# Dense value tiles fetched in pairs, and a rotation of four gather buffers in place of five

## The reference

```python
# expert: (chunk, 8 heads, 16) indices, gate: their softmax weights
u = jnp.take(peer_u, expert, axis=0)
act = jax.nn.gelu(jnp.einsum('chkd,cd->chk', u, zc))
v = jnp.take(peer_v, expert, axis=0)
w = (gate * act.astype(jnp.float32)).astype(zc.dtype)
return jnp.einsum('chk,chkd->cd', w, v).astype(zc.dtype)
```

## Time and profile before

| | us |
|---|---|
| median of 3 runs | 2670.79 (2670.49 to 2677.07) |
| span of the profiled execution | 2671.2 |
| from the first dense matmul to the last | 2281.7 to 2659.0 |
| PE / DVE / ACT / POOL busy, share of the span | 84% / 79% / 43% / 24% |

### The profile page before, as it was taken

How to read it: one execution, slowest core, us unless ns; L and a number is a source line. 1 busy time by engine, 2 the same in 40 slices (tenths; PEclk the granted TensorE clock), 3 DMA queues, 4 the chain that set the end, 5 groups by cost and what they waited for, 6 DMA issues and landing times.

```text
span 2671.2 us, 32182 instructions
## 1 busy us (share of the span) xinstructions
PE 2250.8 (84%) x11476; PEld 1809.5 (68%) x11476; DVE 2099.3 (79%) x2971; ACT 1146.8 (43%) x1721; POOL 639.4 (24%) x834
## 2 busy tenths in 40 slices
PE   8999989999999999989999964444555558999997
PEld 7997778888888888879888841111222225777776
DVE  6986647665566556578766999989999999999997
ACT  5433554443444344453542110000355444548876
POOL 1000000000000000000001353542444442786663
PEclk9999999999999999999999976555677778999999
DMA  6534344555555555545558999999999995899996
GB/s 226 179 129 110 111 157 158 188 189 188 189 188 188 185 186 183 168 128 173 165 167 343 422 420 419 420 419 420 419 417 409 420 418 208 347 405 409 409 409 271
DMA packets 314517, 732.02 MB, mean 274 GB/s; under 512 B 21040, under 2 KB 223024, under 8 KB 275760
## 3 DMA queue, kind: packets, MB, share of 16 engines
q0 software_dynamic: 73728, 402.69, 37.1%
q1 hardware_dynamic: 240544, 327.03, 35.9%
q10 hardware_dynamic: 144, 1.05, 0.1%
HBM read 728.61 MB, written 2.10 MB: 274 GB/s over the span
## 4 chain that ended last, share of the span: by engine, by line
DVE 23%; PE 17%; DMA 13%; issue 3%; POOL 2%; ACT 1%; DVEq 0%; SPq 0%; ACTq 0%; PEldq 0%; POOLq 0%
DVE row L2497 12%; DMA row<-in_peer_u,expert 8%; DMA row<-in_peer_v_rows,expert 5%; PE pg L1294 4%; PE pl L865 4%; PE pl L872 3%; DVE pl L2513 2%; POOL row L801 1%; PE pl L868 1%; PE pl L869 1%; DMA v_tile<-in_peer_v_dense 1%; PE pg L1285 1%; PE pl L1259 1%; PE pl L1188 1%; POOL spread_lo L776 1%
## 5 line engine op out<-in xcount | busy, mean ns | idle before, releaser
L1957 DVE TENSOR_TENSOR wlo<-raw,whi 128x1024 fp32r<-128x1024 f32 (+1 forms) x436 | 517.9, 1208 | 374.9 <-ACT whi L1341 373.3
L1341 ACT ACTIVATE whi<-raw 128x1024 fp32r<-128x1024 f32 (+1 forms) x436 | 444.6, 1039 | 412.0 <-PE pl L872 407.2
L2497 DVE CUSTOM_DVE_ANT_0 row<-row,pg 128x2048 f32<-128x2048 f32 x256 | 574.7, 2284 | 34.0 <-DMA row<-in_peer_u,expert 32.3
L1259 PE MATMUL pl<-row,diag 128*128 128x512 f32 x404 | 316.7, 930 | 333.6 <-DMA row<-in_peer_v_rows,expert 297.8
L865 PE MATMUL pl<-x_split,whi 128*128 128x512 f32 x1888 | 478.5, 395 | 10.2 <-DVE x_split L1965 5.3
L1259 PEld LDWEIGHTS pl<-row,diag 128*128 128x128 f32 x404 | 101.1, 276 | 500.2 <-issue 445.2
L865 PEld LDWEIGHTS pl<-x_split,whi 128*128 128x128 f32 x1888 | 341.5, 190 | 74.6 <-issue 7.5
L872 PE MATMUL pl<-x_split,wlo 128*128 128x256 f32 x2656 | 373.7, 284 | 3.9 <-DVE wlo L1957 3.9
L872 PEld LDWEIGHTS pl<-x_split,wlo 128*128 128x128 f32 x2656 | 359.0, 192 | 23.1 <-DVE wlo L1957 4.5
L801 POOL DMA_INDIRECT row<-in_peer_u,expert x256 | 242.8, 949 | 367.1 <-DVE dots L2497 155.7
L801 POOL DMA_INDIRECT row<-in_peer_v_rows,expert x256 | 261.4, 1021 | 199.4 <-DVE dots L2497 67.0
(11 more groups left out here) (348 smaller groups left out, 3041.6 us busy)
## 6 DMA issues: line engine op xcount, KB each, us to landing
v_tile<-in_peer_v_dense SPq DMA_DIRECT2D x128, 512.0 KB
raw<-in_w_in SPq DMA_DIRECT2D x51, 1024.0 KB
raw<-in_w_gate SPq DMA_DIRECT2D x44, 1024.0 KB
raw<-in_w_up SPq DMA_DIRECT2D x44, 1024.0 KB
raw<-in_w_out SPq DMA_DIRECT2D x32, 1024.0 KB
raw<-in_w_down SPq DMA_DIRECT2D x32, 1024.0 KB
wq<-in_peer_wq SPq DMA_DIRECT2D x15, 1024.0 KB, 11.5
raw<-in_w_down SPq DMA_DIRECT2D x16, 768.0 KB
```

Source lines behind the costliest of these rows:

```text
L1259: last = mm(pl_all[:, c:c + width], diag[:, (at - 1) % 4, :], row[b][:, c - DENSE:c - DENSE + width], start=at == 1, stop=at == ADDED_ROWS ...
L1341: return nc.scalar.activation(o, i, ACT.Copy)
L1957: V.tensor_tensor(wlo[:, n % 4, 0:k, :], w[:, :, f, :], whi[:, n % 4, 0:k, :].bitcast(F32), ALU.subtract)\
L2497: V.tensor_tensor_reduce(row[b][:], row[b][:], z_tok[:], 1.0, 0.0, ALU.mult, ALU.add, dots[:, at:at + 1])\
```

## The change

The dense tiles are read two at a time: 64 transfers of 128 partitions x 2048 float32 (8 KB for each partition, 1 MB each), into three pair buffers that hold six tiles. The table in memory is laid out so that the two tiles of a pair stand next to each other for each partition. One semaphore stands for both tiles of a pair. A pair's buffer is loaded again once PE has finished both of its tiles. To make room, the buffer at `("arena", 3 * D)` leaves the rotation of gathered rows, which has four buffers in this stretch; the homes of `v_hi` move.

```diff
-           43: range(13, 17), SCATTERED: range(17, 18), LATER: range(18, 23)}
+           43: range(13, 17), SCATTERED: range(17, 18), LATER: range(18, 22)}
-ROWS_ALL = 23
+ROWS_ALL = 22
-TILE_HOMES = RING + 1
+PAIR_HOMES = 3
+TILE_HOMES = 2 * PAIR_HOMES
-        homes = [*(("xhi", m * GATHERED) for m in range(4)), ("arena", 3 * D)]
+        homes = [("xhi", m * GATHERED) for m in range(4)]
-        tile_homes = [("arena", 2 * D), ("arena", 3 * D + DENSE), ("arena", 4 * D), ("arena", 4 * D + DENSE),
-                      ("rest", choice_at)]
-        high_homes = [("arena", 2 * D + DENSE), ("rest", choice_at + DENSE), ("rest", choice_at + 2 * DENSE)]
+        pair_homes = [("arena", 2 * D), ("rest", choice_at), ("arena", 4 * D)]
+        tile_homes = [(region, start + h * DENSE) for region, start in pair_homes for h in range(2)]
+        high_homes = [("arena", 3 * D), ("arena", 3 * D + DENSE), ("rest", choice_at + 2 * DENSE)]
-        tile_full = [*slot_full, x_in[0]]
+        pair_full = slot_full[0:PAIR_HOMES]
-            for m in range(NKEY):
-                if m == 2:
+            for q in range(NKEY // 2):
+                if q == 1:
                     sp.wait_ge(hot_used, TT * GROUPS)
                     sp.wait_ge(row_added, ADDED_ROWS)
-                elif m >= TILE_HOMES:
-                    sp.wait_ge(tile_used, m - TILE_HOMES + 1)
+                elif q >= PAIR_HOMES:
+                    sp.wait_ge(tile_used, 2 * (q - PAIR_HOMES + 1))
-                sp.dma_start(v_tile[m % TILE_HOMES][:], A["peer_v_dense"][m]).then_inc(tile_full[m % TILE_HOMES], 16)
+                sp.dma_start(v_pair[q % PAIR_HOMES][:], A["peer_v_dense"][q]).then_inc(pair_full[q % PAIR_HOMES], 16)
-                act.wait_ge(tile_full[m % TILE_HOMES], tile_landed(m))
+                act.wait_ge(pair_full[m // 2 % PAIR_HOMES], tile_landed(m))
-    a["peer_v_dense"] = v[:, 0:DENSE].reshape(NKEY, NKEY, DENSE).transpose(1, 0, 2)
+    v_dense = v[:, 0:DENSE].reshape(NKEY, NKEY // 2, 2, DENSE)
+    a["peer_v_dense"] = v_dense.transpose(1, 0, 2, 3).reshape(NKEY // 2, NKEY, 2 * DENSE)
```

More of the change, by code:

```diff
@@ L99 @@
 ROWS_AT = {0: range(2), 2: range(2, 4), 8: range(4, 6), 20: range(6, 7), 24: range(7, 9), 31: range(9, 11), 37: range(11, 13),
-           43: range(13, 17), SCATTERED: range(17, 18), LATER: range(18, 23)}
+           43: range(13, 17), SCATTERED: range(17, 18), LATER: range(18, 22)}
 ROWS_LEFT = {SCATTERED: (4, 5, 6, 7, 8, 11, 12, 13, 14), LATER: range(18)}
 ROWS_FREE = {2: 1, 8: 2, 20: 4, 24: 5, 31: 6, 37: 7, 43: PH}
-ROWS_ALL = 23
+ROWS_ALL = 22
 ROWS_FROM = {}
-ROWS_SIGNAL = [*range(18), *ROWS_LEFT[SCATTERED][0:5]]
+ROWS_SIGNAL = [*range(18), *ROWS_LEFT[SCATTERED][0:4]]
 def row_buffers():
@@ L347, in build @@
         spread = [spread_all[:, t, 0:NKEY * P].rearrange("p (i c) -> p i c", i=NKEY) for t in range(TT)]
-        tile_homes = [("arena", 2 * D), ("arena", 3 * D + DENSE), ("arena", 4 * D), ("arena", 4 * D + DENSE),
-                      ("rest", choice_at)]
-        high_homes = [("arena", 2 * D + DENSE), ("rest", choice_at + DENSE), ("rest", choice_at + 2 * DENSE)]
-        v_tile = [sb(f"v_tile{m}", region, start, [P, DENSE]) for m, (region, start) in enumerate(tile_homes)]
+        pair_homes = [("arena", 2 * D), ("rest", choice_at), ("arena", 4 * D)]
+        tile_homes = [(region, start + h * DENSE) for region, start in pair_homes for h in range(2)]
+        high_homes = [("arena", 3 * D), ("arena", 3 * D + DENSE), ("rest", choice_at + 2 * DENSE)]
+        v_pair = [sb(f"v_pair{m}", region, start, [P, 2 * DENSE]) for m, (region, start) in enumerate(pair_homes)]
+        v_tile = [v_pair[m // 2][:, m % 2 * DENSE:(m % 2 + 1) * DENSE] for m in range(TILE_HOMES)]
         v_lo = [sb(f"v_lo{m}", region, start, [P, DENSE], F32R) for m, (region, start) in enumerate(tile_homes)]
@@ L533, in tile_landed @@
         def tile_landed(m):
-            n = m % TILE_HOMES
-            earlier = max(LOADS[u] for u in range(len(LOADS)) if u % RING == n) if n < RING else 1
+            n = m // 2 % PAIR_HOMES
+            earlier = max(LOADS[u] for u in range(len(LOADS)) if u % RING == n)
             return 16 * (earlier + m // TILE_HOMES + 1)
@@ L686, in _ @@
             sp.wait_ge(row_added, EARLY)
-            for m in range(NKEY):
-                if m == 2:
+            for q in range(NKEY // 2):
+                if q == 1:
                     sp.wait_ge(hot_used, TT * GROUPS)
                     sp.wait_ge(row_added, ADDED_ROWS)
-                elif m >= TILE_HOMES:
-                    sp.wait_ge(tile_used, m - TILE_HOMES + 1)
-                if m == GAIN_AT:
+                elif q >= PAIR_HOMES:
+                    sp.wait_ge(tile_used, 2 * (q - PAIR_HOMES + 1))
+                if 2 * q == GAIN_AT:
                     sp.dma_start(gain_all[:], A["norm_f_g_2"].rearrange("(a n) -> a n", a=1).broadcast_to([P, D])).then_inc(gain_in, 16)
-                sp.dma_start(v_tile[m % TILE_HOMES][:], A["peer_v_dense"][m]).then_inc(tile_full[m % TILE_HOMES], 16)
+                sp.dma_start(v_pair[q % PAIR_HOMES][:], A["peer_v_dense"][q]).then_inc(pair_full[q % PAIR_HOMES], 16)
             for t in range(TT):
```

## The result

The changed kernel takes 2713.84 us (median of 5 runs, 2705.12 to 2719.88) where the kernel before takes 2670.98 (5 runs): a ratio of 1.0152, with an interval of 1.0137 to 1.0168. By the ratio that is 41 us slower (the medians differ by 43), and outside the predicted range of 2661 to 2693. The profiled execution of the changed kernel took 2705.12 us, 8.7 us less than its median; its span is 2703.3 us, 32.1 us more than that of the profiled execution before.

The account below looks back on a forecast made before the run. The DMA engines were taken to bound the dense stage's long part, PE 2% and DVE 7% behind. 2671.2 - 3.7 (packets) + 2.0 (lumps) gave 2669.5 us profiled, a median of 2669; range 2661 to 2693.

Parts of the forecast that it names:

- Packet size: Dense tile loads: 8 KB packets move at 421 GB/s against 409 for 4 KB, saving 3.7 us on the path.
- A pair lands in 5.3 us: Pair loads: a pair lands about 5.3 us after issue, well inside the 8.8 us allowed; cost 0.
- Two thirds for the pair: Shared DMA engines: packets alternate between queues, so a moving pair gets two thirds; row gathers still fit, only lumpier.
- The landing shrinks with the queue: Four row buffers: landing is mostly queueing, falling from 9.4 to about 7 us, with the DMA engines still setting the pace.
- 2 us for lumps: Dense stage: DMA idle brought by lumpier timing, taken as a doubling of today's gap; 2 us slower.
- The start of the stage: First rows and pair of the dense stage: PE delayed about 1 us, then caught up; cost 0.
- B: Four row buffers: a row's landing stays above 7.9 us and sets the pace; 2692 to 2727 us, chance 0.08.
- A: DVE's row sums: DVE starves for rows while a pair is moving; 19 us slower, 2688 us, chance 0.18.
- The signs: Dense stage profile: DMA share clearly under 1, or over 12 us of PE gaps, would prove the forecast wrong.

Follow-up runs that it names:

- e8: Changed kernel with a fifth row buffer from the 15th row on and a fourth pair buffer from pair 12 on; 2682.92 us.
- e12: e9 with each pair moved as two transfers of 4 KB for each partition on one semaphore; 2677.36 us.
- e9: Changed kernel with a fourth pair buffer from pair 12 on and row buffers growing from four to seven; 2679.61 us.
- e3: Changed kernel with each pair loaded by two 4 KB-per-partition transfers, issued together on the pair's one semaphore; 2711.31 us.
- e11: e2 with two tiles issued at the same moment, each keeping its own 4 KB transfer and semaphore; 2697.65 us.
- e2: Changed kernel's memory map and four row buffers, but six single tiles, each with its own transfer and semaphore; 2690.32 us.
- e13: e10 with each pair moved as two transfers of 4 KB for each partition on one semaphore; 2701.47 us.
- e10: Changed kernel with a fourth pair buffer from pair 12 on, keeping its four row buffers; 2715.77 us.
- e1: Kernel before with four row buffers in the last stretch instead of five, tiles left single; 2689.36 us.
- e4: Changed kernel with the fifth row buffer given back from the 15th row on; 2683.96 us.

## Why the prediction was wrong, step by step

- **Packet size: -3.7 us, wrong.** Pairs did move as 64 transfers of 1024 KB, but no kernel with 8 KB packets moved the predicted 412 to 416 GB/s; the best (e8) had 409 in its long part, where the kernel before had 407. The 421 GB/s of the earlier trace rows were read in a stretch in which one queue did nearly all (q0 has 94.4% of the engines' time from 1500 to 1540 us), so packet size was not the only thing that differed from the dense stage; which of the two made the 421 was not tested. Over half of the traffic here is rows of 4 KB, and e12 against e9 prices the larger packet at no gain.
- **A pair lands in 5.3 us, so it costs 0: wrong.** It landed in 7.4 to 8.5 us on the chain, and ACT's wait grew to 98.9 us instead of shrinking. I costed a pair alone in its queue. But a pair is issued every 6.5 us (2 x 3.23) and needs more than that to land, so it stands behind the one before (argued from these numbers, not tested). Waiting for both halves costs 12 us (e3 against e11); issuing them at once costs 0 to 7 (e11 against e2, not shown).
- **Two thirds for the pair: right as a mechanism, unpriced.** That packets are taken from both queues in turn was read from the earlier trace rows. In the changed kernel the split is not quite two to one: from 2450 to 2453 us q1 (pairs) had 58.8% and q0 (rows) 40.0%. And e13 against e10 shows what that does to the rows: 14 us. I wrote that the sum fits and only the timing is lumpier, and left it at that.
- **The landing shrinks with the queue, the pace stays the engines': the step that failed most.** Of its two halves one held: for single tiles I put 2.6 to 3.1 MB in flight and e1 had 2.8. The other did not. "Still far from an empty queue" had no row behind it. With 2.8 MB the engines moved 389 GB/s, with 2.1 MB 331. A landing of "about 7 us" was 7.8 (median of all rows) in e1, 8.2 on its chain and 8.9 on that of the changed kernel, while the rule of the loop allows 7.65. I also took one landing time for both queues, though rows land 1 us later than tiles (7.8 and 6.8 in e1), and it is the rows that were short.
- **2 us for lumps: mis-sized.** It was the only term of the sum for the lost row buffer and the lumps together. In its place stand 15 us for the lost buffer with single tiles (e1) and 28 with pairs (the changed kernel against e4); 13 us are the pairs' own with five row buffers (e4), and all together are 41.
- **The start of the stage: 0 was wrong** in that what it lost was not made up: PE ran 256 matmuls in the second part against 292, three tiles, 9 us. The reason given (the DMA engines are the bound, so it is caught up) fell with the bound.
- **The rivals.** B was the one that happened, and its own formula would have given it: at 8.88 us a row takes (8.88 + 1.3) / 4 = 2.55 us, 36 us over 152 rows, so 2707 us; the median is 2714, the profiled span 2703. I gave it 0.08, since it was weighed by the same reckoning of the queue as the forecast, so an error there hit both. Its threshold of 7.9 us was also 0.25 too high: POOL's 0.26 us to issue was missing from it, and that alone decided little, as e1 was at 8.2. A's mechanism is there too: DVE waited 49.8 us for rows, at the edge of the 50 that A asked for, and its point, rows held back while a pair moves, is what e13 shows. A and B are one loop: A lengthens the landing, B turns it into time. Taken as separate cases they had 0.26 between them.
- **The signs.** The text named a DMA share clearly under 1 and over 12 us of gaps of PE as proof against it. Both came: 0.97 and 24 us in the long part.

## What to carry to other kernels

When a rotation of buffers gets one shorter, write down the loop: which work stands between one buffer's landing and its next issue, and how many items pass in a turn. Here five rows pass in the landing time plus 3.9 us. Then put in two landing times: the one of now (9.4 us gives 2.66 us a row, 53 us more: the worst) and the one hoped for (7 us gives 2.18, no cost). The truth lay between, at 15 us with single tiles and 41 with pairs. When the two ends decide differently, as here, the forecast must not rest on the hoped one. A change that enlarges the transfers of one queue has to be priced for the other queue that shares the engines, above all if that one has just lost a buffer. The lost buffer alone cost 15 us, the pairs alone (with five or more row buffers) 8 to 13, and both together 41.

## What the runs showed of the hardware

- The DMA share near 1 does not say that the engines are at their rate. In e1 it is 1.00 at 389 GB/s, in the kernel before 1.02 at 407, in the changed kernel 0.97 at 373. Only GB/s beside it tells.
- Transfers of 1 MB were no faster in total than those of 512 KB, with the rows beside them: e9 with 1 MB transfers took 2679.61 us, e12 with 512 KB 2677.36. The Trainium skill (DMA: Bandwidth & Descriptors, "Anatomy of one DMA", for DMAs issued by GpSimd) has a fixed time of about 2 us for each DMA, by which fewer and larger ones would be better. No run here shows that gain; that it is hidden because several transfers are always in flight is my reading, not tested.
- PE's granted clock fell in places. In the changed kernel PE waited 1.84 us for a `v_lo` until 2497.2 us, started again, and from 2498 to 2502 us was granted 0.57, so mostly the lower of its two levels (1.2 and 2.4 GHz):

```profile
2490.00:2498.00 8.00, 6.16 (x27) 4.71 (x26) 6.34 (x6) 5.07 (x7) 5.09 (x6) 1.00 0.99 380
2498.00:2502.00 4.00, 4.00 (x12) 3.12 (x11) 4.00 (x5) 3.90 (x7) 1.95 (x4) 0.57 0.94 347
2502.00:2518.00 16.00, 16.00 (x71) 13.04 (x70) 11.93 (x10) 10.25 (x14) 8.91 (x11) 1.00 0.98 355
```

  So 12 matmuls took 4 us there, where 71 took 16 us right after. Over the stage PE is busy 378.7 us where it was 363.8 for the same work, 15 us more. I take it for a consequence of the slow stage more than for a cause (argued, not tested): e10 shows 0.98 in its long part where the changed kernel shows 0.96, and takes no less time. How much of the 41 us it adds was not measured.
